# Two-layer decoder trunk with expert retrieval: ten query chunks loaded ahead into idle memory, the raw buffers as two more gather slots, and eight picks inside the query projection

## The reference, cut to what matters

```
for l in range(2):
    mod = silu(c) @ ada_w[l] + ada_b[l]          # six vectors of 1024: 48 columns of 128
    h = rms_norm(x) * (1 + scale1) + shift1
    proj = h @ w_in[l]                           # q_a k_a v_a q_b k_b v_b g_a g_b
    y_a = sliding_window_attention(...)          # 8 query heads, rotary, window 128
    y_b = stick_breaking_attention(...)          # 8 heads
    merged = sigmoid(g_a) * (y_a @ w_swa) + sigmoid(g_b) * (y_b @ w_sb)
    x = x + gate1 * (merged @ w_out[l])
    h2 = rms_norm(x) * (1 + scale2) + shift2
    q = h2 @ w_q                                 # 8 heads, 2 halves of 128
    top 16 of 128 sub-keys per half, top 16 of their 256 pair sums: 16 experts per head
    act = gelu(u[experts] . h2);  y = sum(softmax(best) * act * v[experts])
    x = x + gate2 * y
return rms_norm(x)
```

## Time and profile before

| | us |
|---|---|
| median of 3 runs | 1825.43 |
| lowest, highest | 1821.07, 1826.76 |
| the profiled execution | 1823.57 |
| its span in the trace | 1821.4 |

### The profile page before, as it was taken

How to read it: one execution, slowest core, us unless ns; L and a number is a source line. 1 busy time by engine, 2 the same in 40 slices (tenths; PEclk the granted TensorE clock), 3 DMA queues, 4 the chain that set the end, 5 groups by cost and what they waited for, 6 DMA issues and landing times.

```text
span 1821.4 us, 18029 instructions
## 1 busy us (share of the span) xinstructions
PE 1490.5 (82%) x6060; PEld 892.3 (49%) x6060; DVE 1350.4 (74%) x3188; ACT 580.4 (32%) x1286; POOL 507.2 (28%) x556
## 2 busy tenths in 40 slices
PE   2999999878777778778888999997777887788777
PEld 2889987333333333323378988942333333333333
DVE  7897989867777777765578886897777767777555
ACT  3465553222212222322245654432212222222222
POOL 0000023433343333333200000243333433333331
PEclk7999999988999999998999999999899999898999
DMA  9877869999999999999957763899999999999995
GB/s 377 274 244 257 286 235 397 422 422 421 422 422 421 421 421 422 421 421 421 422 219 269 244 209 128 327 392 421 422 421 422 421 421 421 421 421 422 421 422 220
DMA packets 103196, 665.35 MB, mean 365 GB/s; under 512 B 11840, under 2 KB 11968, under 8 KB 32064
## 3 DMA queue, kind: packets, MB, share of 16 engines
q0 software_dynamic: 79488, 578.85, 77.6%
q1 hardware_dynamic: 23616, 85.35, 13.4%
HBM read 663.11 MB, written 1.05 MB: 365 GB/s over the span
## 4 chain that ended last, share of the span: by engine, by line
DMA 46%; PE 31%; DVE 17%; ACT 3%; issue 2%; SPq 0%; DVEq 0%; ACTq 0%
DMA big<-pairs,big 29%; DMA late<-pairs,big 16%; PE yac L670 12%; PE acc L433 10%; PE pg L433 4%; DVE big L1148 3%; DVE wsp L412 2%; DVE late L1148 2%; DVE big L1001 2%; PE acc L555 1%; ACT big L831 1%; DMA big<-ada 1%; ACT wsp L404 1%; DVE big L1067 1%; DVE big L1070 1%
## 5 line engine op out<-in xcount | busy, mean ns | idle before, releaser
L670 PE MATMUL yac<-big 128*128 128x512 f32 x1184 | 571.7, 638 | 142.9 <-ACT big L831 142.9
L670 PE MATMUL yac<-late,big 128*128 128x512 f32 x864 | 418.4, 638 | 116.0 <-ACT big L831 116.0
L670 PEld LDWEIGHTS yac<-big 128*128 128x128 f32 x1184 | 235.5, 204 | 472.0 <-issue 274.3
L1347 POOL DMA_INDIRECT big<-pairs,big x296 | 282.8, 955 | 525.5 <-PE yac L670 409.9
L670 PEld LDWEIGHTS yac<-late,big 128*128 128x128 f32 x864 | 171.0, 203 | 359.5 <-issue 198.2
L1347 POOL DMA_INDIRECT late<-pairs,big x216 | 202.8, 939 | 364.8 <-PE yac L670 311.2
L433 PE MATMUL acc<-hs,wsp 128*128 128x256 f32 x2208 | 284.5, 288 | 6.2 <-ACT big L775 6.1
L433 PEld LDWEIGHTS acc<-hs,wsp 128*128 128x128 f32 x2208 | 271.9, 193 | 11.9 <-ACT big L775 9.4
L1148 DVE CUSTOM_DVE_ANT_0 big<-big,acc 128x1024 f32<-128x1024 f32 x148 | 179.0, 1220 | 112.5 <-DMA big<-pairs,big 112.2
L822 ACT ACTIVATE big<-big 128x4 f32<-128x4 f32 (+1 forms) x138 | 28.3, 205 | 708.8 <-DVE big L1148 708.8
L831 ACT ACTIVATE big<-con,big 128x128 f32<-128x128 f32 x512 | 164.7, 390 | 247.4 <-DVE big L1163 245.6
(11 more groups left out here) (138 smaller groups left out, 1067.4 us busy)
## 6 DMA issues: line engine op xcount, KB each, us to landing
raw<-stream SPq DMA_DIRECT2D x136, 512.0 KB, 4.4
big<-ada_pairs POOLq DMA_DIRECT2D x40, 1024.0 KB, 7.5
...
late<-pairs,big POOLq DMA_INDIRECT x216, 21.6
...
```

The lines of the kernel that those rows point to most:

```text
L670: mm = pe.matmul(yac[:, 2 * t + w, :], diag(n), row(n)[:, D + w * 512:D + (w + 1) * 512], start=(n % (SLOTS // TT) == 0), stop=(n % (SLOTS ...
L1347: g.indirect_dma_start(row(n), None, pairs, bass.IndirectOffsetOnAxis(ap=col(Q_IDX + n).bitcast(U32), axis=0)).then_inc(row_in[n % RING], 16)
```

## The change

- The two padding chunks go, so that SPLITS is 66 and not 68. Value chunks 1 to 4 are multiplied the other way round, two at a time, with the activations as the stationary operand (`v_by_tokens`), which gives tokens by features directly; only value chunk 0 is still transposed. The head's modulation columns move (ADA_FIRST).
- Ten of the sixteen query chunks, 4 to 13, no longer go through `raw`. SP loads them into parts of `big` that are idle between the attention and the picks (`load_early`), at ring loads M_BR+4, +6, +8, +10 and +12 to +17. Only chunks 0 to 3, 14 and 15 stay in the ring.
- The ring of slots grows from 14 to 16; slot 14 lies over raw buffers 0 and 1, slot 15 over 2 and 3. A table SLOT_OF gives the order: first slots 0 to 7, then 14 and 15, then 0 to 3 again. The first use of a slot that holds query chunks waits for their split: slot 0 for chunk 5, 1 for chunk 7, 3 and 4 for chunk 9, 5 for chunk 10, 6 for chunk 12, 7 for chunk 13, 14 for chunk 3, 15 for chunk 15. POOL still issues in one list.
- The retrieval parts stand earlier at the query chunks (TOPK_WQ), and picks 0 to 7 are taken inside the query stage: dots at steps 8 and 10, GELU and weight at 9 and 11, diagonals at 10 and 12, PE's matmuls at 11 and 13.
- Four modulation columns of layer 0 move from the query stage to unit 13 of the picks. The next layer's chunks 0 and 1 are now loaded when slot 14 has been used for the last time (pick 235), 2 and 3 also behind pick 250.

```diff
-ADA_WQ = (0, 0, 4, 5, 10, 11)
-TOPK_WQ = ((1, 0, 0), (2, 0, 1), (3, 0, 2), (3, 0, 3), (6, 1, 0), (7, 1, 1), (8, 1, 2), (9, 1, 3),
-           (12, 2, 0), (12, 2, 1), (13, 2, 2), (13, 2, 3))
+ADA_WQ = (0, 0)
+ADA_UNIT = 13
+TOPK_WQ = ((1, 0, 0), (1, 0, 1), (2, 0, 2), (2, 0, 3), (4, 1, 0), (4, 1, 1), (5, 1, 2), (6, 1, 3),
+           (9, 2, 0), (9, 2, 1), (11, 2, 2), (11, 2, 3))
+DOTS_WQ = (8, 10)
+GATES_WQ = (9, 11)
+GELU_WQ = (9, 11)
+DIAG_WQ = (10, 12)
+PICKS_WQ = (11, 13)
...
+EARLY_WQ = {4: 0, 5: 1, 6: 2, 7: 3, 11: 4, 12: 5, 13: 6, 8: 7, 9: 8, 10: 9}
+EARLY_LOADS = (4, 6, 8, 10, 12, 13, 14, 15, 16, 17)
...
-RING = 14
+RING = 16
+EARLY_IN_SLOT = {0: 5, 1: 7, 3: 9, 4: 9, 5: 10, 6: 12, 7: 13, R_RAW: 3, R_RAW + 1: 15}
...
+            def load_early(L, j):
+                m = M_WQ + list(EARLY_WQ)[j]
+                if j == 0:
+                    sp.wait_ge(av_done, (L + 1) * PAIRS)
+                if m == M_WQ + 8:
+                    sp.wait_ge(pg_free, nth(L, N_BR + N_OUT, 2 + N_BR))
+                if m == M_WQ + 10:
+                    sp.wait_ge(src_done, nth(L, 4 * KD, 3 * KD))
+                sp.dma_start(chunk_raw(L, m), stream[L * SPLITS + m, :, :]).then_inc(early_in[j], 16)
...
-                for n in range(RAW, SPLITS):
+                for n in IN_RING[RAW:]:
                     load_next(L, n)
+                    if n - M_BR in EARLY_LOADS:
+                        load_early(L, EARLY_LOADS.index(n - M_BR))
...
+            def v_by_tokens(L, j):
+                m, e = M_V + 1 + 2 * j, E_V + 1 + 2 * j
+                place = nth(L, SPLITS, m) % W
+                chunk_split(pe, L, m + 1)
                 for t in range(TT):
+                    pe.wait_ge(acc_free, nth(L, EVACS, e + t + 1))
+                    for k in range(KD):
+                        for n, (a, b) in enumerate(TERMS):
+                            mm = pe.matmul(acc[:, (e + t) % 2, 0:2 * P], hs[:, b, k * T + t * P:k * T + (t + 1) * P],
+                                           wsp[:, place:place + 2, a, k * P:(k + 1) * P],
+                                           start=(k == 0 and n == 0), stop=(k == KD - 1 and n == 2))
...
+                    if c == DOTS_WQ[0]:
+                        unit_gates(L, 0)
+                    for g, step in enumerate(DOTS_WQ):
+                        if step == c:
+                            pick_dots(L, g)
+                    for g, step in enumerate(GATES_WQ):
+                        if step == c:
+                            pick_weights(L, g)
                     for step, u, part in TOPK_WQ:
...
                 def gather(n):
-                    if RING_BIG <= n < RING_BIG + W:
-                        pool.wait_ge(chunk_done, (L + 1) * SPLITS + n - RING_BIG + 1)
-                    if n == RING_BIG + W:
+                    r = SLOT_OF[n]
+                    before = USES[r].index(n) - 1
+                    if before >= 0:
+                        pool.wait_ge(slot_done, L * SLOTS + USES[r][before] + 1)
+                    elif r in EARLY_IN_SLOT:
+                        pool.wait_ge(split_done, L * SPLITS + M_WQ + EARLY_IN_SLOT[r] + 1)
+                    elif RING_BIG <= r < RING_BIG + W:
+                        pool.wait_ge(chunk_done, (L + 1) * SPLITS + r - RING_BIG + 1)
+                    elif r >= RING_BIG + W:
                         pool.wait_ge(h2tok_done, L * TT + TT)
```

More of the change, by code:

```diff
@@ L90 @@
 EVACS = E_SK
+EARLY_WQ = {4: 0, 5: 1, 6: 2, 7: 3, 11: 4, 12: 5, 13: 6, 8: 7, 9: 8, 10: 9}
+N_EARLY = len(EARLY_WQ)
+EARLY_LOADS = (4, 6, 8, 10, 12, 13, 14, 15, 16, 17)
+IN_RING = [m for m in range(SPLITS) if m - M_WQ not in EARLY_WQ]
+assert len(IN_RING) % RAW == 0
 assert EVACS % 2 == 0
@@ L99 @@
 SLOTS = UNITS * PICKS
-RING = 14
+RING = 16
 LATE = 6
-RING_BIG = RING - LATE
+RING_BIG = RING - LATE - 2
+R_RAW = RING - 2
+RAW_END = SLOTS - 18
+CYCLE = [0, 1, 2, 3, 8, 9, 4, 5, 6, 7, 10, 11, 12, 13, 15, 14]
+FIRST = list(range(RING_BIG)) + [R_RAW, R_RAW + 1]
+SLOT_OF = FIRST + [r for n, r in sorted(
+    (len(FIRST) + CYCLE.index(r) + RING * t - (min(t, 8) if r in (8, 9) else 0), r)
+    for r in range(RING) for t in range(SLOTS // RING + 2)) if r != R_RAW or n < RAW_END][:SLOTS - len(FIRST)]
+USES = [[n for n in range(SLOTS) if SLOT_OF[n] == r] for r in range(RING)]
 DIAGS = 8
@@ L726, in _ @@
                         h2_by_tokens(0)
+                    for g, step in enumerate(PICKS_WQ):
+                        if step == c:
+                            for n in range(*GROUP_OF[g]):
+                                add_pick(L, n)
                 head_subkeys(L, 7)
```

214 lines of the change are left out of this document (129 added, 85 removed).

## The result

The changed kernel takes 1837.3 us (median of 4 runs, 1836.0 to 1840.2) against 1824.5 us (median of 4, 1821.1 to 1826.8) before: ratio 1.0078, 95% interval 1.0061 to 1.0095. The execution profiled took 1837.62 us and has a span of 1835.8, 14.4 more than before. The prediction was 1835.

A forecast was written before the change was run, and what follows sets the result against it. DMA engines were taken to bound the picks, PE and DVE the projections ahead. 1823.57 + 8.6 + 5.9 (query stages) - 4.8 (value stage) + 2 (output projection) = 1835.3, say 1835 us; range 1827 to 1844.

The forecast's parts named there:

- What bounds the kernel: DMA engines set the pace in the picks at 421 GB/s; PE and DVE set it in the projections ahead.
- Query stage, the chain: DVE's list in the query stage, layer 0: index ready at 255.2 us, split 15 done at 297.5, releasing gather 9.
- Query stage, the size: Fewer gather bytes moved by 299.4 us: +8.6 us in layer 0 (7 to 10), +5.9 in layer 1 (4.5 to 7.5).
- The break-even: Query stage: each microsecond gather 9 comes sooner is worth one a layer; about 6 us sooner in both layers breaks even.
- The first rival: Query stage: gather 9 isn't late and the DMA engines run without a gap, giving 1795.6 us; chance 0.10.
- Value stage: Head projections: no padding products, fewer transposes and copies, shorter PE stall at the head scores; 2.4 us a layer, -4.8.
- My test: Value stage: the forecast is wrong if the products of L645 take more than 3 us for 24.
- Clock: Value stage: the shorter stall may keep PE's full clock; by the skill's page the sum would be 3 us lower.
- another 1.5 us: Value stage, a bound: the further gain if the shorter stall leaves PE at 2.4 GHz, not 1.2.
- Output projection: Layer 0, 196 to 220 us: early loads meet modulation columns that come just in time; +2 us, from 0 to +4.
- Gather time: Query stage: a gather takes at least 5.5 us from issue to landing; the skill's page would give 4.4.

The follow-up runs named there:

- parts_late: The changed kernel with unit 2's four retrieval parts moved behind more query-chunk splits, gather 9 still in the raw slot: 1826.1 us.
- slot15_late: The changed kernel with the second raw slot (slot 15) used at its turn in the cycle, not as gather 9: 1817.4 us.
- no_early_picks: The changed kernel with picks 0 to 7 put back behind the query chunks: 1838.2 us.
- values_alone: The kernel before with values by tokens and the head's modulation columns at their new places, padding chunks kept: 1822.7 us.
- slot15_loads: slot15_late with the last four early loads issued later, and one more by a single place: 1815.6 us.
- six_early: slot15_loads with six query chunks loaded early instead of ten, another slot order, and both raw slots out of the first turn: 1810.6 us.

## Why the prediction was right

- **What bounds the kernel.** Right. The picks run at 421 GB/s as before, and each MB not moved before the gap-free stretch is paid in full.
- **Query stage, the chain.** Right in its order, and close in its times. From the split of chunk 4 to the first gather I had 12.9 us; it took 13.4 (240.03 to 253.43). From there to gather 9 I had 42.3; it took 43.2 in both layers. Dot 7 waited 2.6 us, not 2.1. Nine gathers' worth had moved when gather 9's data began: 9.54 MB, against 9.44.
- **Query stage, the size.** Mis-sized a little. From the split of chunk 4 (240.03 against 242.26, -2.2) to layer 0's last dot (924.82 against 916.70, +8.1) the loss is 10.4 us, where the sum had 8.6 and its bound 10. Gather 9 in its list explains 0.9 and the index 0.5 (0.4 of that lie between DVE's last index instruction and the gather, which my list had at nothing). The last 0.4 stand behind gather 9: from 298.5 to 313 us the rate was 404 GB/s and not 421, so the dip of the earlier trace rows had not gone whole. In layer 1 the last dot moved by 6.2 us more, and the value stage had given 1.9, which makes 8.1, against 5.9 and a bound of 7.5. There 1.4 us go the same way as in layer 0, and 0.9 stand ahead of the list: the split of chunk 4 waited 2.76 us for ACT, where before had 1.82. Both layers lie outside the bounds that I gave them.
- **The break-even.** "At about 6 us sooner in both layers": parts_late had 6.3 and 6.6, and came out 2.4 us above before. Right to some 2 us. The price of a microsecond was 0.87, not 1.
- **The first rival** (gather 9 not late, 1795.6). Its premise was made true in slot15_late, and the time was 1817.4. It took every slot to be free as soon as gather 9 was. In fact splits still gate gathers 3 to 7, and DMA share is 0.81 and 0.75 for 40 us.
- **Value stage.** The number was right and its cause wrong. The stall's product came at 84.38 (foreseen: 85.3), 2.4 us earlier once the 0.9 us by which the stage began sooner (57.52 against 58.44) are off, and 1.9 us in layer 1; DVE's first score step stood at 78.64. I had ascribed this mostly to transposes and copies saved by the new form. The step that failed is "Gone are the padding products and eight of ten transposes": I priced two edits as one. Dropping the padding gave 2.3 us in layer 0, through two splits fewer in DVE's list; the new form took 1.0 away, and the moved columns gave perhaps 1.1. That the whole came out at 2.4, the number forecast, is luck. My test, products of L645 over 3 us for 24, was badly chosen too: they take 3.05 (6.10 for 48 at 58.20), much as the head projections do (6.01 for 48 at 75.80), and the form is still the slower one, through DVE.
- **Clock.** At the stall the 24 products took 3.13 us, not the 4.63 of the earlier trace rows, with 1.00 granted from 84 to 96 us. The Trainium skill, "TensorE: Matmul & The Clock Gate", Part 1, has activity release the clock, and the trace agrees here: the stall was 1.71 us and not 2.55. But the "another 1.5 us" of the bounds, and the 3 us less that I drew from the Trainium skill, didn't come. Two products on, before and then now:

```profile
96.79 3.14 PE L433 MATMUL acc<-hs,wsp 128*128 128x256 f32 x24
```

```profile
93.46 3.13 PE L476 MATMUL acc<-hs,wsp 128*128 128x256 f32 x24 [1.00 <-ACT big L860]
```

  That is 3.33 us earlier, exactly as at the stall: a new wait took back what the clock gave. Layer 1 reads the same (0.99 us, 1.9 earlier at both places). PE's pace didn't bound this stretch. Nor is the clock safe behind a stall of this length. In no_early_picks the same stall of 1.71 us in layer 1 was followed by the row below, and in values_alone a stall of 2.22 us was followed by 24 products in 3.10 us in layer 0 and in 4.49 in layer 1, though the stretch of the table is equally long in both.

```profile
985.20 4.64 PE L476 MATMUL acc<-hs,wsp 128*128 128x256 f32 x24 [1.71 <-ACT big L860]
```

- **Output projection.** Right in kind: DVE's wait for a column went from 0.34 to 2.20 us. Of the 2 us in the sum, 1.1 reached the query stage (POOL's loads were 3.3 us ahead of before at 212 us, DVE's split of chunk 4 was 2.2 us ahead).
- **Gather time.** The shortest from issue to landing is 5.3 us in slot15_loads and 5.6 in six_early, like the 5.5 of the earlier trace rows; in the changed kernel dot 7 starts 5.75 us behind the issue of its gather. The Trainium skill, "DMA: Bandwidth & Descriptors", "Anatomy of one DMA — SWDGE (gpsimd) path", gave 4.4, an estimate; the measurement decides.

The total was closer than its terms, and that is luck: their errors had opposite signs. The measured sum is -0.9 (start), -2.4 and -1.9 (value stage), +1.1 (output projection), +10.4 and +8.1 (query stages), +0.1 (end), 14.4 us in all; the forecast's was 11.7. The query stages cost 4 us more and the value stage gave 0.5 less; the output projection and the start gave 1.8 back.
